# VectorE's row operations move behind the halves of a group: a parallel mixer block with a product-key expert layer

## The chip, the cores and the metric

The kernel runs on one core of a Trainium2 chip. The metric is the device time of one execution in microseconds (us): three runs of the kernel before gave 1671.1, 1673.12 and 1674.15 us, with a median of 1673.12. One further execution was taken with the hardware profiler; every row below is from it. The engines are TensorE (PE in the rows; PEld is its weight load), VectorE (DVE), ScalarE (ACT), GpSimd (POOL) and SyncE (SP), which only issues transfers.

## The reference

One layer over 512 tokens of width 1024 in float32: a convolution branch and a recurrent branch are mixed and added to `x`, and then an expert layer chooses, for each token, 128 of 16384 experts (8 heads with 16 each). The change lies in the expert layer alone, which is

```python
h = rmsnorm(x, norm_ffn_g[l])
...
def block(args):                                   # xt tokens, et their experts, gt their gates
    xt, et, gt = args
    u_sel = jnp.take(u_tab, et, axis=0)
    act = jax.nn.gelu(jnp.einsum('tkd,td->tk', u_sel, xt), approximate=False)
    v_sel = jnp.take(v_tab, et, axis=0)
    return jnp.einsum('tk,tkd->td', gt * act, v_sel)
...
return rmsnorm(x + peer_ffn(...), norm_f_g)
```

## The kernel before, in words

All the convolution, recurrence, routing and the weights of the experts are done before the main loop, which begins at about 884 us and lasts to about 1666 us of the span. Two ways of computing the expert layer run beside each other in it.

*Dense, on TensorE.* For 352 of the 512 tokens every expert is computed. The 16384 experts are 128 blocks of 128, and four blocks (`G`) are a group; the loop has 32 groups (`NG`), with numbers q from 0 to 31. For two of the four blocks the scores have been computed before the loop (`gl`, loaded from DRAM); for the other two they are computed in it (`ge`). TensorE does, for group q: `unit(q, 0)`, `unit(q, 1)`, `scores` of group q+1's third block, `unit(q, 2)`, `unit(q, 3)`, `scores` of group q+1's fourth block. A unit is 18 matmuls, a `scores` is 24 matmuls of which the last 8 read `uL`. The last group has no `scores`, and its very last unit ends with four matmuls that add the rest sum `accX` through `fold`; they wait until all row operations are done (`row_used`).

Products are done in pairs of halves: a high half made by ScalarE (`uH`, `vH`, `aH`) and a low half, the difference, made by VectorE (`uL`, `vL`, `aL`). For a block g of group q VectorE does `weigh` (writes `af`, the scores after Gelu times the gates), `v_low` (writes `vL`) and `a_low` (writes `aL`); a unit waits for `vL` and `aL`. For a block in the loop `weigh` waits for ScalarE's Gelu `ge`, and the Gelu of the fourth block waits for the `scores` that TensorE does last before `unit(q, 0)`. A `scores` waits for `u_low` (writes `uL`) before its last 8 matmuls.

*Sparse, on VectorE.* For the other 160 tokens only the chosen experts are computed: GpSimd gathers rows of `u_tab` and `v_tab` by indirect DMA, 128 rows of 4 KB at a time, into a ring of ten buffers (`ring`, `SR` is 10). In an even step VectorE does ten dot products with them (`dot`, into `spd`), ScalarE puts them through Gelu (`spg`), in the next, odd step VectorE weighs them (`gate`, writes `spa`) and adds ten gathered rows of `v_tab` times these weights into `accs` and, for the last two, `accX` (`add_row`). `row(k)` is a dot product in an even step and an addition in an odd one. Each row operation frees its buffer, and GpSimd's next gather into that buffer waits for it. An `add_row` also waits for the row operation before it:

```python
dve.wait_ge(row_used, 2 * SR * i + SR + k)
```

SyncE loads the blocks of `u_tab` and `v_tab` (512 KB each), the gates `wg` and the scores `gl` as their buffers are freed by the low halves.

Every engine executes its instructions in the order in which they are written; semaphores alone order the engines. VectorE's order for a group is written out by hand in `step`, with the row operations between the halves.

*The end.* When all row operations are done ScalarE takes the sum of squares of `accs` (`square_sum(0, DT, ...)`), and then, in this order, those of TensorE's three tiles of tokens as each is done (`tile_done`). Each is followed by a square root, VectorE's reciprocal and the last scaling into `yo`, and a store.

Of the kernel before, what the change touches and what calls it, by code (L numbers as in the profile page):

```python
# [76 lines left out]
G = 4  # L77
# [10 lines left out]
NPRE = PRE * NG  # L88
# [3 lines left out]
SR = SM + SX  # L92
# [6 lines left out]
def build(nc, xT, xR, consts, smalls, sels, reset, vecs, wlora, wall, w2a2, g2, keysT, uT, u_tab, v_tab, gfrow,  # L99
# [228 lines left out]
    with ExitStack() as ctx:  # L328
# [1371 lines left out]
        def _(dve):  # L1700
# [532 lines left out]
            def u_low(n, slot):  # L2233
                dve.wait_ge(uh_ready, n + 1)
                tt(uL[:, slot % 2, :, :], uraw[:, slot, :, :], uH[:, slot % 2, :, :], ALU.subtract).then_inc(
                    ul_ready, 1)
# [26 lines left out]
            def weigh(i, par, g):  # L2263

                q = 2 * i + par
                if g == 0:
                    dve.wait_ge(wg_loaded[par], 32 * i + 16)
                if g >= PRE:
                    dve.wait_ge(gelu_ready, NPRE + 2 * q + g - PRE + 3)
                dve.wait_ge(al_ready, G * q + g + 1)  # L2270
                src = gl[:, par, g, :] if g < PRE else ge[:, g - PRE, :]
                tt(af[:, g % 2, :].rearrange("p (b t) -> p b t", t=T_W), src.rearrange("p (b t) -> p b t", t=T_W),  # L2272
                   wg[:, par, :, g, :], ALU.mult).then_inc(act_ready, 1)

            def a_low(q, g):
                dve.wait_ge(ah_ready, G * q + g + 1)
                tt(aL[:, g, :], af[:, g % 2, :], aH[:, g, :], ALU.subtract).then_inc(al_ready, 1)

            def v_low(q, g):
                if g in POOL_V:  # L2280
                    return
                dve.wait_ge(vh_ready, G * q + g + 1)
                tt(vL[:, g, :], vraw[:, g, :], vH[:, g, :], ALU.subtract).then_inc(vl_dve, 1)  # L2283
# [4 lines left out]
            def dot(i, k):  # L2288

                dve.wait_ge(row_loaded[k], 32 * i + 16)  # L2290
                row, x = (ring[k][:, :], h2T[:, :]) if k < SM else (by_chunk_of_d(ring[k]), h2X)
                stt(row, row, 1.0, x, ALU.mult, ALU.mult, accum_out=spd[:, k:k + 1]).then_inc(row_used, 1)  # L2292

            def gate(i):
                dve.wait_ge(sp_gelu, i + 1)
                tt(spa[:, 0:SM], spg[:, 0:SM], best[:, DT].rearrange("p a b -> p (a b)")[:, bass.ds(SM * i, SM)],
                   ALU.mult)
                tt(spa[:, SM:], spg[:, SM:], gtx[:, bass.ds(SX * i, SX)], ALU.mult).then_inc(sp_gated, 1)  # L2298

            def add_row(i, k):  # L2300

                dve.wait_ge(row_loaded[k], 32 * i + 32)
                if k == 0:
                    dve.wait_ge(sp_gated, i + 1)
                dve.wait_ge(row_used, 2 * SR * i + SR + k)
                row, total = (ring[k][:, :], accs[:, :]) if k < SM else (by_chunk_of_d(ring[k]), accX)
                stt(total, row, spa[:, k:k + 1], total, ALU.mult, ALU.add).then_inc(row_used, 1)  # L2307
# [12 lines left out]
            def step(i, par, more):  # L2320
                q = 2 * i + par
                base = 2 * (1 - par)

                def row(k):
                    if par == 0:
                        dot(i, k)
                    else:
                        add_row(i, k)

                weigh(i, par, 0)  # L2330
                v_low(q, 0)
                a_low(q, 0)
                if not par:
                    row(0)
                weigh(i, par, 1)
                if not par:
                    row(1)
                v_low(q, 1)
                a_low(q, 1)
                if par:  # L2340
                    gate(i)
                    row(0)
                    row(1)
                row(2)
                weigh(i, par, 2)
                row(3)
                v_low(q, 2)
                a_low(q, 2)
                row(4)
                if more:  # L2350
                    u_low(NPRE + 2 * (q + 1), base)
                row(5)
                weigh(i, par, 3)
                v_low(q, 3)
                row(6)
                a_low(q, 3)
                row(7)
                if more:
                    u_low(NPRE + 2 * (q + 1) + 1, base + 1)
                row(8)  # L2360
                row(9)

            with dve.Fori(0, NG // 2 - 1) as i:
                step(i, 0, True)
                step(i, 1, True)
            step(NG // 2 - 1, 0, True)
            step(NG // 2 - 1, 1, False)

# [229 lines left out]
```

## Time and profile before

| | us |
|---|---|
| median of three runs (lowest, highest) | 1673.12 (1671.1, 1674.15) |
| the profiled execution, its own time | 1673.59 |
| its span | 1671.8 |
| TensorE busy in the span | 1661.5 (99%) |
| VectorE busy | 1437.0 (86%) |
| ScalarE busy | 724.1 (43%) |
| GpSimd busy | 757.7 (45%) |
| mean granted clock of TensorE | 0.998 |

The profiled execution's own time is 1.79 us over its span. The shares are those of the whole span, of which the first half is not the loop; the rows below are read by stage. A row of the timeline has a start, a duration, the engine, the line, the operation, what it writes and reads and how many instructions are merged in it, and in brackets the idle time of the engine before it with what ended it.

### The profile page before, as it was taken

Reading aid. Unit: us, or ns where it says so; the run is one execution under the profiler, and the core shown is the slowest. Engines: PE = TensorE matmul, PEld = TensorE weight load, DVE = VectorE, ACT = ScalarE, POOL = GpSimd, SP = SyncE. Lnnn points to the kernel's source line nnn. Section 1 sums busy time; section 2 is a strip of 40 time slices with the busy share of each in tenths; the row PEclk is TensorE's granted clock in tenths of the full one; section 3 lists DMA queues with packets and bytes.
Section 4 is the critical chain, followed back from the end, with each engine's and each line's share of the span. In section 5 each row is a group of like instructions: output and inputs, shape, how many; then the busy total and the mean of one; then the engine's idle time right before and its main releaser. Section 6 shows DMA issues by size and latency. Waiting matters only on the chain.

```text
span 1671.8 us, 33592 instructions
## 1 busy us (share of the span) xinstructions
PE 1661.5 (99%) x12009; PEld 1435.8 (86%) x12009; DVE 1437.0 (86%) x2759; ACT 724.1 (43%) x1053; POOL 757.7 (45%) x605
## 2 busy tenths in 40 slices
PE   9999999999999999999999999999999999999998
PEld 6878788788888999999998888888888888888886
DVE  5379988666598999999997999999999999999996
ACT  5565445453422333467774434343333333333333
POOL 0000000010054477688885665655555565555550
PEclk9999999999999999999999999999999999999999
DMA  5221122244322355578889999999999999999993
GB/s 188 79 74 53 47 90 78 84 176 149 116 81 85 131 184 175 185 223 255 253 261 367 410 410 410 410 410 410 409 394 394 385 385 383 387 384 401 393 350 112
DMA packets 166339, 424.98 MB, mean 254 GB/s; under 512 B 14160, under 2 KB 75728, under 8 KB 166000
## 3 DMA queue, kind: packets, MB, share of 16 engines
q1 hardware_dynamic: 117328, 244.52, 41.0%
q0 software_dynamic: 48928, 179.33, 27.8%
q8 instruction: 55, 0.90, 0.2%
q14 instruction: 28, 0.23, 0.0%
HBM read 382.87 MB, written 39.45 MB: 253 GB/s over the span
## 4 chain that ended last, share of the span: by engine, by line
PE 97%; ACT 1%; DVE 1%; issue 0%; DVEq 0%; ACTq 0%
PE unit L453 97%; DVE oneh L2220 0%; PE unit L608 0%; ACT L1241 0%; PE unit L1030 0%; ACT ld L1241 0%; ACT aa L1241 0%; ACT k L1241 0%; ACT best L1241 0%; ACT pk L1241 0%; DVE wL L1720 0%; ACT sqj L1241 0%; ACT wst L1241 0%; ACT kn L1241 0%; ACT uH L1241 0%
## 5 line engine op out<-in xcount | busy, mean ns | idle before, releaser
L453 PE MATMUL unit<-h2H,uH 128*128 128x352 f32 x1024 | 334.7, 328 | 0.2 <-ACTq L1572 0.2
L453 PE MATMUL unit<-h2L,uH 128*128 128x352 f32 x1024 | 328.8, 323 | 0.0
L2440 POOL DMA_INDIRECT ring<-u_tab,idx x128 | 172.6, 1348 | 156.1 <-DVE accs L2307 122.3
L453 PE MATMUL unit<-vL,aH 128*128 128x512 f32 (+1 forms) x768 | 241.7, 396 | 0.0
L453 PE MATMUL unit<-vH,aH 128*128 128x512 f32 (+1 forms) x768 | 239.4, 392 | 0.0
L453 PE MATMUL unit<-vH,aL 128*128 128x512 f32 (+1 forms) x768 | 238.9, 392 | 0.0
L2440 POOL DMA_INDIRECT ring<-v_tab,idx x128 | 172.6, 1348 | 139.1 <-DVE ring L2292 132.6
L453 PEld LDWEIGHTS unit<-h2H,uH 128*128 128x128 f32 x1024 | 192.8, 188 | 4.6 <-issue 0.4
L453 PEld LDWEIGHTS unit<-h2L,uH 128*128 128x128 f32 x1024 | 193.0, 188 | 2.8
L453 PE MATMUL unit<-h2H,uL 128*128 128x352 f32 x1024 | 191.2, 325 | 0.0
L1241 ACT ACTIVATE vH<-vraw 128x1024 fp32r<-128x1024 f32 x128 | 135.0, 1055 | 91.0 <-PE unit L453 91.0
L453 PEld LDWEIGHTS unit<-vH,aL 128*128 128x128 f32 (+1 forms) x768 | 137.8, 179 | 41.5
L453 PEld LDWEIGHTS unit<-vL,aH 128*128 128x128 f32 (+1 forms) x768 | 137.6, 179 | 40.0
L1241 ACT ACTIVATE aH<-af 128x352 fp32r<-128x352 f32 x128 | 63.4, 495 | 244.7 <-DVE af L2272 244.6
L1241 ACT ACTIVATE ge<-unit 128x352 f32<-128x352 f32 x128 | 58.7, 459 | 253.0 <-PE unit L453 252.3
L2307 DVE SCALAR_TENSOR_TENSOR accs<-ring,spa,accs 128x1024 f32<-128x1024 f32 x128 | 164.0, 1281 | 4.8 <-DVE spa L2298 3.3
L453 PEld LDWEIGHTS unit<-h2H,uL 128*128 128x128 f32 x1024 | 167.8, 189 | 0.0
L453 PEld LDWEIGHTS unit<-vH,aH 128*128 128x128 f32 (+1 forms) x768 | 135.9, 179 | 32.3
L2283 DVE TENSOR_TENSOR vL<-vraw,vH 128x1024 fp32r<-128x1024 f32 x128 | 156.0, 1219 | 8.2 <-ACT vH L1241 8.2
L2387 POOL DMA_DIRECT2D gate_dram<-gst x16 | 8.9, 555 | 332.6 <-ACT gst L1241 332.6
L2292 DVE SCALAR_TENSOR_TENSOR ring<-ring,h2T 128x1024 f32<-128x1024 f32 x128 | 155.7, 1217 | 0.3 <-DMA ring<-u_tab,idx 0.3
L2463 POOL TENSOR_SCALAR oh<-cst,e2s 128x128 f32<-128x128 f32 x176 | 136.0, 787 | 14.2 <-PE unit L453 12.9
(331 smaller groups left out, 3309.1 us busy)
## 6 DMA issues: line engine op xcount, KB each, us to landing
uraw<-uT SPq DMA_DIRECT2D x128, 512.0 KB, 6.4
vraw<-v_tab SPq DMA_DIRECT2D x128, 512.0 KB, 7.6
wraw<-wall SPq DMA_DIRECT2D x68, 512.0 KB, 3.3
w_dram<-wst SPq DMA_DIRECT2D x11, 1920.0 KB, 8.6
wg<-w_dram SPq DMA_DIRECT2D x30, 704.0 KB, 7.0
g_dram<-ge SPq DMA_DIRECT2D x64, 176.0 KB, 1.9
gl<-g_dram SPq DMA_DIRECT2D x32, 352.0 KB, 9.0
gate_dram<-gst POOLq DMA_DIRECT2D x16, 256.0 KB, 2.3
```

What stands on the lines that cost most here:

```text
L453: return pe.matmul(out, lhsT, rhs, start=start, stop=stop, skip_group_check=True)
L1241: return act.activation(out, in_, f, **kw)
L2283: tt(vL[:, g, :], vraw[:, g, :], vH[:, g, :], ALU.subtract).then_inc(vl_dve, 1)
L2292: stt(row, row, 1.0, x, ALU.mult, ALU.mult, accum_out=spd[:, k:k + 1]).then_inc(row_used, 1)
L2307: stt(total, row, spa[:, k:k + 1], total, ALU.mult, ALU.add).then_inc(row_used, 1)
L2387: pool.dma_start(gate_dram[k], gst[:, k % 2, :]).then_inc(gate_stored[k % 2], 16)
L2440: pool.indirect_dma_start(out=ring[k][:, :], out_offset=None, in_=(u_tab, v_tab)[half], in_offset=bass.IndirectOffsetOnAxis(ap=rows[:, m:m ...
L2463: ins = pool.tensor_scalar(oh2[:, b, k, :], C(C_IOTA), e2s[:, tok:tok + 1], None, ALU.is_equal)
```

## The change

`step` on VectorE is written in another order; no instruction's work is changed, and no other engine's program. Three groups of operations that stood between each other are separated: `gate` and both `u_low` come behind the four blocks' `weigh`, `v_low` and `a_low`, and the row operations behind these, all ten in an odd step (`par` is 1). In an even step four of the ten stay between the blocks, one behind each `a_low`, and six come at the end. Inside a block `v_low` stands ahead of `a_low` as before.

```diff
-                weigh(i, par, 0)
-                v_low(q, 0)
-                a_low(q, 0)
-                if not par:
-                    row(0)
-                weigh(i, par, 1)
-                if not par:
-                    row(1)
-                v_low(q, 1)
-                a_low(q, 1)
+                for g in range(G):
+                    weigh(i, par, g)
+                    v_low(q, g)
+                    a_low(q, g)
+                    if par == 0:
+                        row(g)
                 if par:
                     gate(i)
-                    row(0)
-                    row(1)
-                row(2)
-                weigh(i, par, 2)
-                row(3)
-                v_low(q, 2)
-                a_low(q, 2)
-                row(4)
                 if more:
-                    u_low(NPRE + 2 * (q + 1), base)
-                row(5)
-                weigh(i, par, 3)
-                v_low(q, 3)
-                row(6)
-                a_low(q, 3)
-                row(7)
-                if more:
-                    u_low(NPRE + 2 * (q + 1) + 1, base + 1)
-                row(8)
-                row(9)
+                    for s in range(2):
+                        u_low(NPRE + 2 * (q + 1) + s, base + s)
+                for k in range(0 if par else G, SR):
+                    row(k)
```

The first place is VectorE's last step of the program, group 31, an odd one without `u_low`. `ring_201` to `ring_204` are the last four of the ten gathered buffers. Before, from the fourth block's `weigh` to the last addition:

```order
L2272 TENSOR_TENSOR af<-ge,wg 128x352
L2283 TENSOR_TENSOR vL<-vraw,vH 128x1024
L2307 SCALAR_TENSOR_TENSOR accs<-ring_201,spa,accs 128x1024
L2277 TENSOR_TENSOR aL<-af,aH 128x352
L2307 SCALAR_TENSOR_TENSOR accs<-ring_202,spa,accs 128x1024
L2307 SCALAR_TENSOR_TENSOR accX<-ring_203,spa,accX 128x8x128
L2307 SCALAR_TENSOR_TENSOR accX<-ring_204,spa,accX 128x8x128
```

And now, from the same `weigh`:

```order
L2272 TENSOR_TENSOR af<-ge,wg 128x352
L2283 TENSOR_TENSOR vL<-vraw,vH 128x1024
L2277 TENSOR_TENSOR aL<-af,aH 128x352
L2296 TENSOR_TENSOR spa<-spg,best 128x8
L2298 TENSOR_TENSOR spa<-spg,gtx 128x2
L2307 SCALAR_TENSOR_TENSOR accs<-ring_195,spa,accs 128x1024
L2307 SCALAR_TENSOR_TENSOR accs<-ring_196,spa,accs 128x1024
L2307 SCALAR_TENSOR_TENSOR accs<-ring_197,spa,accs 128x1024
L2307 SCALAR_TENSOR_TENSOR accs<-ring_198,spa,accs 128x1024
L2307 SCALAR_TENSOR_TENSOR accs<-ring_199,spa,accs 128x1024
L2307 SCALAR_TENSOR_TENSOR accs<-ring_200,spa,accs 128x1024
L2307 SCALAR_TENSOR_TENSOR accs<-ring_201,spa,accs 128x1024
```

Behind the fourth block's `weigh` there stood four additions; now there stand all ten (the three after the last row shown are those of `ring_202`, `ring_203` and `ring_204`).

The second place is VectorE's last even step, group 30, from the third block's `weigh`. Before:

```order
L2272 TENSOR_TENSOR af<-ge,wg 128x352
L2292 SCALAR_TENSOR_TENSOR ring_198,spd<-ring_198,h2T 128x1024
L2283 TENSOR_TENSOR vL<-vraw,vH 128x1024
L2277 TENSOR_TENSOR aL<-af,aH 128x352
L2292 SCALAR_TENSOR_TENSOR ring_199,spd<-ring_199,h2T 128x1024
L2235 TENSOR_TENSOR uL<-uraw,uH 128x1024
L2292 SCALAR_TENSOR_TENSOR ring_200,spd<-ring_200,h2T 128x1024
```

And now:

```order
L2272 TENSOR_TENSOR af<-ge,wg 128x352
L2283 TENSOR_TENSOR vL<-vraw,vH 128x1024
L2277 TENSOR_TENSOR aL<-af,aH 128x352
L2292 SCALAR_TENSOR_TENSOR ring_197,spd<-ring_197,h2T 128x1024
L2272 TENSOR_TENSOR af<-ge,wg 128x352
L2283 TENSOR_TENSOR vL<-vraw,vH 128x1024
L2277 TENSOR_TENSOR aL<-af,aH 128x352
L2292 SCALAR_TENSOR_TENSOR ring_198,spd<-ring_198,h2T 128x1024
L2235 TENSOR_TENSOR uL<-uraw,uH 128x1024 x2
L2292 SCALAR_TENSOR_TENSOR ring_199,spd<-ring_199,h2T 128x1024
```

The first `uL`, for which TensorE's `scores` waits, stood behind five dot products and three blocks; now it stands behind four dot products and four blocks.

## Rows read from the trace of the kernel before

**Rows 1.** Engines in two stretches of the loop: busy time of PE, PEld, DVE, ACT, POOL; clock; DMA; GB/s
```profile
900.00:1000.00 100.00, 100.00 (x496) 84.89 (x496) 95.83 (x129) 35.39 (x52) 67.24 (x49) 1.00 1.03 410
1300.00:1400.00 100.00, 100.00 (x492) 84.32 (x491) 92.31 (x124) 35.17 (x51) 56.40 (x42) 1.00 1.00 386
```

**Rows 2.** The chain of waits: start, length, what, for the whole loop
```profile
883.68 782.54 PE unit L453 x3844
```

**Rows 3.** Timeline of PE: first matmuls of a group, of a scores, of a group
```profile
891.20 0.63 PE L453 MATMUL unit<-vH,aH 128*128 128x512 f32 x2
...
1208.38 0.62 PE L453 MATMUL unit<-vH,aH 128*128 128x512 f32 x2
...
1216.72 0.32 PE L453 MATMUL unit<-h2H,uH 128*128 128x352 f32 x1
...
1232.78 0.62 PE L453 MATMUL unit<-vH,aH 128*128 128x512 f32 x2
```

**Rows 4.** Timeline of DVE: first step, an even step, and the odd one's gate
```profile
885.80 0.53 DVE L2272 TENSOR_TENSOR af<-gl,wg 128x352 f32<-128x352 f32 x1 [1.01 <-DMA wg<-wst]
...
1217.64 0.52 DVE L2272 TENSOR_TENSOR af<-gl,wg 128x352 f32<-128x352 f32 x1
...
1219.64 1.22 DVE L2292 SCALAR_TENSOR_TENSOR ring<-ring,h2T 128x1024 f32<-128x1024 f32 x1
...
1220.79 0.52 DVE L2272 TENSOR_TENSOR af<-gl,wg 128x352 f32<-128x352 f32 x1
...
1233.56 0.53 DVE L2272 TENSOR_TENSOR af<-ge,wg 128x352 f32<-128x352 f32 x1 [1.82 <-ACT ge L1241]
1234.42 1.23 DVE L2283 TENSOR_TENSOR vL<-vraw,vH 128x1024 fp32r<-128x1024 f32 x1 [0.33 <-ACT vH L1241]
...
1246.84 0.17 DVE L2296 TENSOR_TENSOR spa<-spg,best 128x8 f32<-128x8 f32 x1 [1.03 <-ACT spg L1241]
...
1247.34 3.93 DVE L2307 SCALAR_TENSOR_TENSOR accs<-ring,spa,accs 128x1024 f32<-128x1024 f32 x3 [0.22 <-DVE spa L2298]
```

**Rows 5.** Timeline of ACT beside the same fourth block
```profile
1232.98 0.46 ACT L1241 ACTIVATE ge<-unit 128x352 f32<-128x352 f32 x1 [6.54 <-PE unit L453]
...
1235.23 0.49 ACT L1241 ACTIVATE aH<-af 128x352 fp32r<-128x352 f32 x1
```

**Rows 6.** DMA issues of 960 to 1100 us: out<-in, count, median us to landing
```profile
ring<-u_tab,idx POOLq DMA_INDIRECT x24, 18.2
```

**Rows 7.** The same of 1300 to 1500 us
```profile
ring<-u_tab,idx POOLq DMA_INDIRECT x36, 6.9
```

**Rows 8.** Timeline of DVE in its last step
```profile
1636.59 4.07 DVE L2307 SCALAR_TENSOR_TENSOR accs<-ring,spa,accs 128x1024 f32<-128x1024 f32 x3
...
1648.35 0.53 DVE L2272 TENSOR_TENSOR af<-ge,wg 128x352 f32<-128x352 f32 x1 [1.90 <-ACT ge L1241]
...
1650.45 1.28 DVE L2307 SCALAR_TENSOR_TENSOR accs<-ring,spa,accs 128x1024 f32<-128x1024 f32 x1
1651.64 0.52 DVE L2277 TENSOR_TENSOR aL<-af,aH 128x352 fp32r<-128x352 f32 x1
```

**Rows 9.** Timeline of PE: the last matmuls
```profile
1664.30 1.90 PE L453 MATMUL unit<-accX,fold 128*32 128x512 f32 x4
```

**Rows 10.** Timeline of ACT at the end
```profile
1656.16 1.06 ACT L1241 ACTIVATE sqj<-accs 128x1024 f32<-128x1024 f32 x1 [6.51 <-DVE accX L2307]
...
1657.33 1.28 ACT L1241 ACT_TABLE_LOAD   x1
1658.63 0.29 ACT L1241 ACTIVATE rsf<-ssq,vec 128x1 f32<-128x1 f32 x1
1661.62 1.03 ACT L1241 ACTIVATE sqj<-unit 128x1024 f32<-128x1024 f32 x1 [2.70 <-PE unit L453]
...
1663.02 1.03 ACT L1241 ACTIVATE sqj<-unit 128x1024 f32<-128x1024 f32 x1
...
1666.24 1.02 ACT L1241 ACTIVATE sqj<-unit 128x1024 f32<-128x1024 f32 x1 [1.78 <-PE unit L453]
```

## The prediction, made before the changed kernel was run

> **What bounds the kernel now.** I read the page first for the shares, then the engines by stretch, then the chain of waits, then the timelines of one even and one odd step, and last those of the end.
>
> In both stretches of the loop TensorE is busy for 100.00 of 100 us at a granted clock of 1.00, its full 2.4 GHz [rows 1], and the chain holds it in one unbroken piece of 782.54 us, from 883.68 to 1666.22 us [rows 2]. So the loop is TensorE's alone. From one first unit to the next is 1232.78 - 1208.38 = 24.40 us; two units take 1216.72 - 1208.38 = 8.34, so four take 16.68 and each of the two scores 3.86 [rows 3]. VectorE is at 92 to 96% in the loop [rows 1]: it isn't the bound, but has only about 2 us in 24.4 to give. The reader is to see two things. No reordering on VectorE can make the loop shorter, since TensorE does not wait there. And VectorE runs ahead: for the group that TensorE begins at 1232.78 it began at 1217.64, a lead of 15.1 us [rows 3, 4]. That lead was only 891.20 - 885.80 = 5.4 us at the first group. It ends where the fourth block's weigh must wait for the Gelu of scores which TensorE finishes just before the group (1.82 us idle, at 1233.56, 0.78 us behind TensorE's start) [rows 4].
>
> **The change, part by part.** It removes and adds no work: 10 row operations, 4 blocks and 2 uL per step, as before. Three costs are possible: TensorE waits for a half that comes later; the rows cost more when they stand together; and the last rows end later. All are worked out from the pinned point, TensorE's start B of a group.
>
> *An odd step.* The fourth weigh starts at B + 0.78, its vL at B + 1.64 [rows 4], aH ends at 1235.23 + 0.49, so B + 2.94 [rows 5], and aL, the last instruction of the blocks, at about B + 3.4. Two small multiplications of the gate take 0.50 (1246.84 to 1247.34). Then come two uL, for which I take a dot product's pitch, 1220.79 - 1219.64 = 1.15, since they work on as many elements: B + 6.2. Then ten additions. Their pitch differs by what stands between: three in a row take 3.93, of which the last is 1.28 long, so (3.93 - 1.28) / 2 = 1.33 [rows 4], while one with another instruction behind it gives way after 1651.64 - 1650.45 = 1.19 [rows 8]. An addition waits for the one before, and this wait is hidden when something else stands between. Ten together: 9 x 1.33 + 1.2 = 13.2, about 1 us more than interleaved. The step ends at B + 19.4, and VectorE begins the next, even group 24.4 - 19.4 = 5.0 us before TensorE does, no longer 15.
>
> *An even step.* Weigh, vL and aL of a block take 1219.64 - 1217.64 = 2.00 [rows 4]. The first aL is ready 2.1 us after the step's start, 2.9 us before its unit. Four blocks (8.0), four dots (4.6) and the first uL (1.2) take 13.8 us, so uL is there at 8.8 us of TensorE's group. TensorE reads it after two units and 16 of the 24 score matmuls, 8.34 + 2/3 x 3.86 = 10.9. This slack of 2.1 us is the smallest in the loop. The second block has 2.9 + 4.17 - 1.15 - 2.0 = 3.9 of slack, the later ones more. With the second uL and six dots the step ends 8.0 + 4.6 + 2.3 + 6.9 = 21.8 us after its start, and the odd step begins 24.4 + 5.0 - 21.8 = 7.6 us ahead of TensorE. Its first three blocks take 6 us, with perhaps 1 us of wait for vH, and then VectorE idles until the Gelu. So both steps are pinned again, the 1 us of dearer additions is taken from VectorE's idle time, and TensorE never waits. The leads, 5.0 and 7.6, are near the 5.4 with which the loop begins, so the start needs no time of its own. Cost of the loop: 0. The cover is 2.1 us; beyond it each late microsecond in an even step is paid 16 times.
>
> *The end.* Here nothing covers. Before, rows were done when ScalarE began to square accs, at 1656.16, long before TensorE's last matmul [rows 10]. Now the fourth weigh still starts at 1648.35 and vL ends its turn at 1650.45 [rows 8]; aL (0.45) and the gate (0.4) bring 1651.3; ten additions follow. In this step, which stands outside the loop, the pitch of dependent ones is (4.07 - 1.28) / 2 = 1.39 [rows 8], so they end at 1651.3 + 9 x 1.39 + 1.28 = 1665.1. ScalarE is then the chain: from squaring accs to its root are 1658.63 - 1656.16 = 2.47 us, with the table load of 1.28 in it that was hidden before, the root 0.29, and two tiles of 1663.02 - 1661.62 = 1.40 each [rows 10]. The third tile's square starts at 1665.1 + 2.47 + 0.29 + 2.80 = 1670.7 in place of 1666.24: 4.4 us later. The last matmuls, four of 1.90 us in all, wait for the rows too, from 1665.1 in place of 1664.30 [rows 9], but end at 1667.0, before ScalarE wants them. What lies behind the third square (root, reciprocal, scaling, store) stays, only that the stores now follow each other by 1.40 us; one of 512 KB takes 1.36 us at 386 GB/s [rows 1], so they barely queue: 0.1, with 0 to 0.5 as bounds.
>
> The Trainium skill (VectorE: DVE Perf Modes, The DRAIN you can't avoid) has it that the gap between two VectorE operations is the pipeline's own and that a semaphore on each costs nothing more. The trace has 1.39 against 1.19 for the additions that wait for each other. By the page the pitch in the end would be the shorter one; that is the second rival below.
>
> The Trainium skill (ScalarE: Activation LUTs, What ACT_TABLE_LOAD costs) charges a change of table about 2.66 us, 1.28 of load and 1.38 of drain. The load's 1.28 agrees, but the root starts 0.02 us behind it [rows 10]. If the drain came in as well now that the load is on the path, the sum would be 1.4 us more; this is the last rival.
>
> *Sum.* 4.4 + 0.1 = 4.5 us on the profiled execution's 1673.59, so 1678.1. That execution stood 0.47 over the median of the runs, so for the median 1677.6 us.
>
> **The rivals.**
>
> *Rows land too late, and TensorE starves.* A buffer freed by the first addition at about B + 7.5 is wanted by the first dot product of the even step at B + 19.4 + 2.0 = 21.4: 13.9 us for issue and landing. In 960 to 1100 us a gather landed 18.2 us after its issue [rows 6], which would be 4.3 late, 2.2 beyond the slack. In 900 to 1200 us, six pairs of steps, that is 13 us: 1691, and if it held to the end 16 x 2.2 = 35. Against it: this delay is a queue. It stood while VectorE ran faster than TensorE and pulled 410 GB/s; later, pinned, it asks for 386 and a gather lands in 6.9 us [rows 1, 7], 7 us inside the limit. The change pins VectorE from the first pairs on. If it hits the first pairs only, 2 to 7 us: about 1682. A wait of TensorE might also lower its clock, which is nowhere below 1.00 in these stretches.
>
> *The rows end early enough (the other side).* If in the last step the additions follow each other by 1.19, they end at 1651.3 + 9 x 1.19 + 1.28 = 1663.3, the third square starts at 1668.9, and the loss is 2.6 us: 1675.7, no measurable change. The point from which it decides: nothing is lost at all if the rows end by 1666.24 - 5.56 = 1660.7, and under 0.2% if by 1664.0. For it: single additions do this. Against it: the three rows in this very step did not.
>
> *A gain in the loop.* Only if TensorE had waits that the profile doesn't show; with 782.54 unbroken I give it little.
>
> *The table's drain:* 4.5 + 1.4 = 5.9, or 1679.0.
>
> **How the numbers follow.** Forecast 0.67; late rows 0.10; short pitch 0.16; gain 0.03; drain 0.04. 0.2% is 3.3 us, about what a measurement of this kernel can tell from no change; the border is 1676.5. The forecast's own spread is about 1 us each way (noise of the medians, the gate and aL read to 0.3, the stores), so a tenth of it falls within 0.2%. Slower: 0.60 + 0.10 + 0.04 = 0.74; same: 0.07 + 0.16 = 0.23; faster 0.03. The range takes in the short pitch below and the mild case of late rows above: 1675.5 to 1681.5.
>
> **What the profile after would show.** TensorE's period still 24.40, at clock 1.00, and no idle in the loop. VectorE's lead about 5 us in even and 7.6 in odd steps, and idle before the fourth weigh in odd steps only. Gathers landing in 7 to 10 us already around 1000 us. VectorE's last addition ending near 1665, ScalarE squaring accs right behind it, and the third tile's square near 1670.7. The forecast is wrong if the chain shows VectorE or a gather inside the loop, or if ScalarE's squares of the first two tiles start when their tiles are done.

## The result, and the profile after

| | before | after |
|---|---|---|
| median of the runs, us (lowest, highest) | 1672.8 (1671.1, 1674.15), 6 runs | 1679.72 (1678.54, 1680.96), 6 runs |
| ratio to before, 95% interval | | 1.0036 (1.0026 to 1.0047) |
| profiled execution, own time / span | 1673.59 / 1671.8 | 1680.04 / 1678.2 |
| VectorE, GpSimd busy | 1437.0, 757.7 | 1446.7, 724.4 |

By the ratio the change makes the kernel slower by 6.0 us (4.4 to 7.9 by the interval; the medians in the table lie 6.9 apart); the forecast was 4.5. Experiment 1 and two pairs of profiles below put the loss into the last step.

*The loop.* The engines by stretch, the same two as in [rows 1], in the profile after (busy time of PE, PEld, DVE, ACT, POOL; clock, DMA share, GB/s):

```profile
900.00:1000.00 100.00, 100.00 (x494) 84.56 (x493) 94.09 (x125) 34.70 (x51) 56.85 (x46) 1.00 1.03 410
1300.00:1400.00 100.00, 100.00 (x492) 84.38 (x491) 93.02 (x124) 35.57 (x53) 52.69 (x43) 1.00 1.01 388
```

TensorE is as full as before. Its timeline has the first unit of the first group, of an odd and an even group, the first matmul of the even group that reads `uL`, and the first unit of the last group:

```profile
892.83 0.63 PE L453 MATMUL unit<-vH,aH 128*128 128x512 f32 x2
...
1210.01 0.62 PE L453 MATMUL unit<-vH,aH 128*128 128x512 f32 x2
...
1234.41 0.62 PE L453 MATMUL unit<-vH,aH 128*128 128x512 f32 x2
...
1245.31 1.45 PE L453 MATMUL unit<-h2H,uL 128*128 128x352 f32 x8
...
1649.21 0.62 PE L453 MATMUL unit<-vH,aH 128*128 128x512 f32 x2
```

From the first unit to the last group's are 756.38 us, or 31 groups of 24.40, the period of [rows 3]. The kernel before has the same length, 1647.58 - 891.20 = 756.38; its last group begins at

```profile
1647.58 0.62 PE L453 MATMUL unit<-vH,aH 128*128 128x512 f32 x2
```

VectorE beside these groups (the `weigh` of the odd group's fourth block, its additions, the even step's first `weigh`, its `uL`, the next step's first `weigh`):

```profile
1210.79 0.53 DVE L2272 TENSOR_TENSOR af<-ge,wg 128x352 f32<-128x352 f32 x1 [1.82 <-ACT ge L1241]
...
1215.84 10.52 DVE L2307 SCALAR_TENSOR_TENSOR accs<-ring,spa,accs 128x1024 f32<-128x1024 f32 x8
...
1228.92 0.52 DVE L2272 TENSOR_TENSOR af<-gl,wg 128x352 f32<-128x352 f32 x1
...
1241.53 2.35 DVE L2235 TENSOR_TENSOR uL<-uraw,uH 128x1024 fp32r<-128x1024 f32 x2
...
1250.68 0.51 DVE L2272 TENSOR_TENSOR af<-gl,wg 128x352 f32<-128x352 f32 x1
```

The even step begins 1234.41 - 1228.92 = 5.5 us ahead of TensorE; in [rows 3, 4] this lead was 15.1. The next odd step begins 1234.41 + 24.40 - 1250.68 = 8.1 us ahead. The gathers land sooner in 960 to 1100 us (median landing times; the first was 18.2 in [rows 6]):

```profile
ring<-u_tab,idx POOLq DMA_INDIRECT x24, 8.9
ring<-v_tab,idx POOLq DMA_INDIRECT x23, 11.7
```

Ahead of that, in 884 to 960 us, those of `u_tab` still took 12.5 us, against 14.7 in the kernel before. VectorE waited for a gather three times in the whole loop, 2.8 us in all (3.7 before), and TensorE never.

*The end.* The chain of waits on the profile's page, which was TensorE for 97% of the span before, now holds nothing of TensorE (engine shares of the whole span):

```profile
DVE 1%; issue 0%; ACT 0%; DVEq 0%
```

The chain is followed back from the last instruction, and here it breaks off at the gate of the last step, at 1652.59 us; its shares say nothing of what lies ahead of that, where TensorE is as busy as before (99% of the span). What the chain does show is that the last 25 us belong to VectorE and ScalarE. VectorE, ScalarE and TensorE there:

```profile
1649.98 0.53 DVE L2272 TENSOR_TENSOR af<-ge,wg 128x352 f32<-128x352 f32 x1 [2.76 <-ACT ge L1241]
...
1652.84 11.02 DVE L2307 SCALAR_TENSOR_TENSOR accs<-ring,spa,accs 128x1024 f32<-128x1024 f32 x8
1663.97 2.67 DVE L2307 SCALAR_TENSOR_TENSOR accX<-ring,spa,accX 128x1024 f32<-128x1024 f32 x2
...
1673.90 1.41 DVE L2358 SCALAR_TENSOR_TENSOR yo<-unit,rsf,gfb 128x512 f32<-128x512 f32 x2
```

```profile
1666.68 1.06 ACT L1241 ACTIVATE sqj<-accs 128x1024 f32<-128x1024 f32 x1 [15.39 <-DVE accX L2307]
...
1667.84 1.28 ACT L1241 ACT_TABLE_LOAD   x1
1669.14 0.29 ACT L1241 ACTIVATE rsf<-ssq,vec 128x1 f32<-128x1 f32 x1
1669.34 1.00 ACT L1241 ACTIVATE sqj<-unit 128x1024 f32<-128x1024 f32 x1
...
1671.99 1.00 ACT L1241 ACTIVATE sqj<-unit 128x1024 f32<-128x1024 f32 x1
```

```profile
1666.70 1.90 PE L453 MATMUL unit<-accX,fold 128*32 128x512 f32 x4 [0.70 <-DVE accX L2307]
```

Before, ScalarE squared `accs` at 1656.16 and then waited for TensorE's tiles [rows 10]. Now it starts at 1666.68 with all tiles but the last finished, and nothing between the square of `accs` and the third tile's waits for TensorE. TensorE's last group began 1.63 us later in this profile (1649.21 against 1647.58), so the comparison is made from there: the third square starts 22.78 us behind it, where it was 1666.24 - 1647.58 = 18.66: 4.12 us. From that square to the end of the span are 1678.2 - 1671.99 = 6.21 us against 5.56: 0.65 more. Together 4.8. The other 1.6 of the spans' 6.4 lies ahead of the loop.

Of the 0.65, 0.24 is VectorE's: its last scaling starts 1673.90 - 1671.99 = 1.91 behind the square, where it was 1667.91 - 1666.24 = 1.67, because it is still scaling the second tile. The kernel before has for the same scaling

```profile
1667.91 1.41 DVE L2377 SCALAR_TENSOR_TENSOR yo<-unit,rsf,gfb 128x512 f32<-128x512 f32 x2
```

The other 0.41 lies behind the scaling. The last two stores, halves of the third tile, land 2.5 us (median) after their issue where they took 2.0; first the kernel before, then the change:

```profile
y<-yo SPq DMA_DIRECT2D x2, 256.0 KB, 2.0
...
y<-yo SPq DMA_DIRECT2D x2, 256.0 KB, 2.5
```

### The profile page after: what moved, and what is told of

The parts are those of the page before. It is cut to its first block and busy times, and to the rows that moved or that the text cites. A ratio compares the mean times of both kernels' runs of the same rounds, so it can differ in the third digit from the quotient of the medians.

```text
span 1678.2 us, 33592 instructions
## 1 busy us (share of the span) xinstructions
PE 1661.5 (99%) x12009; PEld 1436.5 (86%) x12009; DVE 1446.7 (86%) x2759; ACT 717.3 (43%) x1053; POOL 724.4 (43%) x605
## 5 line engine op out<-in xcount | busy, mean ns | idle before, releaser
L2421 POOL DMA_INDIRECT ring<-v_tab,idx x128 | 186.0, 1453 | 154.1 <-DVE ring L2292 135.5
L2421 POOL DMA_INDIRECT ring<-u_tab,idx x128 | 142.8, 1116 | 195.2 <-DVE accs L2307 143.2
L2292 DVE SCALAR_TENSOR_TENSOR ring<-ring,h2T 128x1024 f32<-128x1024 f32 x128 | 152.2, 1214 | 1.5 <-DMA ring<-u_tab,idx 1.5
L2412 POOL TENSOR_TENSOR uL<-uraw,uH 128x1024 fp32r<-128x1024 f32 x42 | 113.8, 2712 | 61.2 <-ACT uH L1241 61.2
```

What stands on the lines that cost most here:

```text
L2412: pool.tensor_tensor(uL[:, slot % 2, :, :], uraw[:, slot, :, :], uH[:, slot % 2, :, :], ALU.subtract).then_inc(ul_ready, 1)
L2421: pool.indirect_dma_start(out=ring[k][:, :], out_offset=None, in_=(u_tab, v_tab)[half], in_offset=bass.IndirectOffsetOnAxis(ap=rows[:, m:m ...
```

## The experiments

The experiments ran in three series, each on one chip and with the kernel before in it, and a ratio is to the runs of that kernel in the same series. The change itself ran again only in the first series (experiments 1 to 3), where it measured 1.0033. Experiments 4 to 7 are compared with that number across series. Where the text adds up a trace, it takes two stretches as above: from TensorE's first unit of the last group to the third tile's square (18.66 in the kernel before), and from there to the end of the span (5.56).

**1. The last step alone, both ways.** The new order everywhere but in the last step:

```diff
-                for g in range(G):
-                    weigh(i, par, g)
-                    ...
+                if more:
+                    ...                       # the new order
+                else:
+                    ...                       # the order of before
```

> The new order in all steps but the last (group 31), which has the order of before. Theory of the end (the loss is the ten additions behind the last block, which put ScalarE's squares behind them): no loss, within 1.5 us of before; the third tile's square again right behind its last matmul. Rival, the loop or what lies ahead of it (TensorE began the last group 1.6 us later in the profile of the change): 1.5 to 2 us slower than before, with no waits in the end.

Measured 1.0005 (0.9996 to 1.0014). And the reverse, the old order everywhere but in the last step:

> The order of before in all steps but the last (group 31), which has the new one. Theory of the end: the whole loss, 4.8 us over before (4.1 until the third square starts, 0.65 behind it). Rival, loop or before it: 4.8 less than the change as a whole by 1.5 to 2, so about 3 to 4 over before if the change as a whole is 6.

Measured 1.0034 (1.0022 to 1.0046), beside 1.0033 (1.0021 to 1.0045) for the whole change in the same series. In the profile of this second kernel the third square starts 22.79 us behind the last group's start and the span ends 6.27 later, as in the change. So the last step makes the whole loss by itself, and the 31 reordered steps alone cost 0.05%, at most 0.14%. The rival, a part in the loop or ahead of it, falls by the traces: from the first unit to the last group's are 756.37 us in both kernels, and the end of the second costs 4.8. The intervals by themselves (-0.7 to 2.3 us for the first kernel) would still admit its 1.5 to 2.

The first kernel's profile has something that I did not look for. TensorE's first unit of its last group, and ScalarE at its end:

```profile
1650.23 0.62 PE L453 MATMUL unit<-vH,aH 128*128 128x512 f32 x2
...
1663.60 1.06 ACT L1241 ACTIVATE sqj<-accs 128x1024 f32<-128x1024 f32 x1 [6.25 <-DVE accX L2307]
...
1666.26 1.01 ACT L1241 ACTIVATE sqj<-unit 128x1024 f32<-128x1024 f32 x1
...
1668.92 1.00 ACT L1241 ACTIVATE sqj<-unit 128x1024 f32<-128x1024 f32 x1
```

The rows end 1663.60 - 1650.23 = 13.4 us behind the start of the group, where in the kernel before they ended 8.6 behind it, although the last step is the same. The short lead is carried into the last step: VectorE arrives late and has no idle time left in it. The third square still starts 18.7 us behind TensorE's start, just as before, but the three squares now follow each other without a gap, so by these rows any later end of the rows would move it. And what lies behind it is already dearer: from the third square to the end of the span are 1675.2 - 1668.92 = 6.28 us in place of 5.56, with scalings and stores as close together as in the change. So by the trace the reordered loop is not quite free: its shorter lead costs 0.7 us in the end even with the old last step, which agrees with the 1.0005 (0.8 us) measured. The whole change has the same 0.7 once, not twice.

**2. The change once more, and the kernel before once more.**

> The change once more, as it is. Theory of the end: 4.8 us over before, plus noise of about 1. Rival with a part ahead of the end: 6 again, and in the profile TensorE's last group again begins 1.6 us later than in the kernel before, at about 1649.2 us. If that start lies elsewhere this time, it is a difference between executions.

> The kernel before once more, for a second profile. If the 1.6 us by which the last group began later in the profile of the change is a difference between executions, this one may begin its last group anywhere from about 1647 to 1650 us, with the main loop's length unchanged; if it belongs to the change, it begins at 1647.6 again.

The change: 1.0033 (1.0021 to 1.0045); its profile has 891.50 for the first unit of the loop and 1647.87 for the first unit of the last group, 756.37 between them. The kernel before, one execution of 1674.32 us:

```profile
891.93 0.63 PE L453 MATMUL unit<-vH,aH 128*128 128x512 f32 x2
...
1656.89 1.06 ACT L1241 ACTIVATE sqj<-accs 128x1024 f32<-128x1024 f32 x1 [6.52 <-DVE accX L2307]
...
1666.97 1.02 ACT L1241 ACTIVATE sqj<-unit 128x1024 f32<-128x1024 f32 x1 [1.78 <-PE unit L453]
```

In this second pair the loop of the change begins 0.43 us before that of the kernel before (891.50 against 891.93), in the first pair it began 1.63 after it (892.83 against 891.20). Over all twelve profiles of this study the first unit starts between 889.84 and 893.86 us, in kernels whose instructions ahead of it are the same. So the 1.6 us are a difference between executions and no fixed cost of the change. Two profiles of the kernel before are too few to say whether the changed ones begin later by some tenths on average.

The end costs the same in both pairs. In the second profile of the kernel before the last group begins at 1648.30, and the third square follows 18.67 behind it; in the change's second profile the third square is at 1670.66, 22.79 behind the last group's start. From there to the end of the span are 5.53 and 6.24: together 4.8 again.

**3. The order of ScalarE's squares.**

```diff
-            act.wait_ge(row_used, P // SM * 2 * SR)
-            square_sum(0, DT, accs[:, :])
-            for t in range(DT):
-                act.wait_ge(tile_done, t + 1)
-                square_sum(t + 1, t, ...)
+            for n, t in enumerate((0, 1, DT, 2)):
+                if t == DT:
+                    act.wait_ge(row_used, P // SM * 2 * SR)
+                else:
+                    act.wait_ge(tile_done, t + 1)
+                square_sum(n, t, ...)          # DT is accs
```

The same order is given to VectorE's scaling and SyncE's stores, in two lines left out here.

> The change, with ScalarE squaring tiles 0 and 1 first, then accs, then tile 2 (VectorE's scaling and the stores in the same order). Theory of the end: the table load and two squares go back under TensorE's last matmuls; rows still end 17.4 us behind TensorE's start of the group, accs is squared from there, tile 2 1.4 later, 0.9 later than in the kernel before: 1 to 1.5 us over before, 3.3 less than the change. Rival, that the rows' end itself or the last four matmuls that wait for it are the loss: no more than 1 us less than the change.

Its profile has, for TensorE's first unit of the last group and its last matmuls, and for ScalarE's third tile:

```profile
1649.45 0.62 PE L454 MATMUL unit<-vH,aH 128*128 128x512 f32 x2
...
1666.94 1.90 PE L454 MATMUL unit<-accX,fold 128*32 128x512 f32 x4 [0.69 <-DVE accX L2309]
```

```profile
1668.88 1.02 ACT L1242 ACTIVATE sqj<-unit 128x1024 f32<-128x1024 f32 x1
```

Measured 1.0016 (1.0007 to 1.0025), 2.7 us over before and 2.8 under the change of the same series. The mechanism holds: rows end as late as in the change, and half of the loss is gone or more, because two squares are done before the rows end or beside them. The third tile's square starts 1668.88 - 1649.45 = 19.43 us behind the group's start, 0.77 later than before; that part was forecast well. The expected 1 to 1.5 us over before was low by the part behind it: 1675.5 - 1668.88 = 6.62 us from that square to the end, as against 5.56, 0.6 of it because VectorE is still scaling `accs` (its last scaling starts 2.29 us behind the square, not 1.67). By the trace the kernel is 1.8 us over before, within the interval of the runs (1.2 to 4.2).

**4. The table load.**

```diff
+            fn(rsf[:, 0:1], vc("eps", 0), ACT.Sqrt)
             def square_sum(n, t, src):
```

> The change, with one square root of a constant on ScalarE behind its last aH, so that the table of the root is loaded while the rows are still added. Theory of the end: 1.3 us less than the change (the load alone, its drain is not on the path), so 3.5 us over before, and the third tile's square starts 4.0 us behind the accs square in place of 5.3. Rival, the drain belongs to the load: 2.7 less. Rival, the load comes back at the next square: no gain.

```profile
1650.77 1.28 ACT L1241 ACT_TABLE_LOAD   x1
...
1666.15 1.06 ACT L1241 ACTIVATE sqj<-accs 128x1024 f32<-128x1024 f32 x1 [13.88 <-DVE accX L2309]
...
1667.53 1.00 ACT L1241 ACTIVATE sqj<-unit 128x1024 f32<-128x1024 f32 x1
...
1670.35 1.00 ACT L1241 ACTIVATE sqj<-unit 128x1024 f32<-128x1024 f32 x1
```

Measured 1.0021 (1.0012 to 1.0030). From the accs square to the third tile's are 4.20 us, against 1671.99 - 1666.68 = 5.31 with the load in between: 1.1 less, near the load's 1.28 and far from 2.7. Between the accs square and the first tile's the whole 1.28 is gone (1667.53 - 1666.15 = 1.38 in place of 1669.34 - 1666.68 = 2.66); 0.15 comes back between the next two, for a reason that I did not find. The load is not done again. No drain was on the path: in the change the root starts 0.02 us behind the load. By the trace the kernel is 3.5 us over before (21.68 and 6.05), as forecast. The times, also 3.5 us, agree with that, but 0.12% under the change's 1.0033 of another series could not have told 1.1 from 2.7.

**5. Both.** The early load with the order of experiment 3.

> The same early load, and ScalarE squares tiles 0 and 1 first, then accs, then tile 2. Theory of the end: accs is squared right behind the rows (17.5 us behind TensorE's start of the group) and tile 2 1.3 us later, 0.1 to 0.2 later than in the kernel before; VectorE's scaling and the stores, closer together, add 0.6 to 0.9: within 1.1 us of before, 3.7 less than the change. Rival, the rows themselves are the loss through the last four matmuls: still 2 us or more over before.

```profile
1666.24 1.06 ACT L1242 ACTIVATE sqj<-accs 128x1024 f32<-128x1024 f32 x1 [0.59 <-DVE accX L2311]
...
1668.20 1.02 ACT L1242 ACTIVATE sqj<-unit 128x1024 f32<-128x1024 f32 x1 [0.49 <-PE unit L454]
```

Measured 1.0007 (0.9998 to 1.0016), 1.2 us. The detail I had wrong: the third square was to follow at once, and it waits 0.49 us for TensorE. The last four matmuls wait for the rows as well, end 1.90 us after them, and now that ScalarE is out of the way they are what is late. The third square so starts 1668.20 - 1648.77 = 19.43 us behind the group's start, where 0.1 to 0.2 over 18.66 was expected, and the span ends 6.60 behind it: 1.8 us over before by the trace, the same as experiment 3 with its 19.43 and 6.62. There ScalarE and the last four matmuls (1666.94 + 1.90 = 1668.84) are ready together, so taking the load away uncovers nothing but them. That the early load adds to the order of experiment 3 is therefore not shown: the 1.5 us between the two ratios lie within their intervals, and the traces have none of it. Some three fifths of the loss are gone by the trace, four fifths by the runs, without moving a row. This kernel isn't faster than the one before either, and none in this study is.

**6. How long additions take side by side.** In the last step alone:

```diff
-            def add_row(i, k):
+            def add_row(i, k, place=None, back=0):
...
-                dve.wait_ge(row_used, 2 * SR * i + SR + k)
+                dve.wait_ge(row_used, 2 * SR * i + SR + (k if place is None else place) - back)
...
+                if not more:
+                    for place, k in enumerate((0, 8, 1, 9, 2, 3, 4, 5, 6, 7)):
+                        add_row(i, k, place, 1 if 0 < place < 5 else 0)
+                    return
```

> The change, with the ten additions of the last step alone in another order: rows 0, 8, 1, 9, 2 and then the rest, so that neighbours write different sums, and each of the second to fifth waits only for the addition before the last. Theory that the longer pitch is the wait for the neighbour's end: those four start 1.2 us after their neighbour instead of 1.39, and accs is squared 0.8 us earlier. Rival, that the gap belongs to two long operations back to back whatever they wait for: 1.39 for all. The time moves by less than 1 us either way.

```profile
1652.49 1.29 DVE L2307 SCALAR_TENSOR_TENSOR accs<-ring,spa,accs 128x1024 f32<-128x1024 f32 x1
1653.69 1.28 DVE L2307 SCALAR_TENSOR_TENSOR accX<-ring,spa,accX 128x1024 f32<-128x1024 f32 x1
1654.89 1.28 DVE L2307 SCALAR_TENSOR_TENSOR accs<-ring,spa,accs 128x1024 f32<-128x1024 f32 x1
1656.09 1.28 DVE L2307 SCALAR_TENSOR_TENSOR accX<-ring,spa,accX 128x1024 f32<-128x1024 f32 x1
1657.28 8.22 DVE L2307 SCALAR_TENSOR_TENSOR accs<-ring,spa,accs 128x1024 f32<-128x1024 f32 x6
```

The four that don't wait for their neighbour start 1.20 us after it; the six that do take 8.22, or (8.22 - 1.28) / 5 = 1.39 each. `accs` is squared 13.05 us behind the first addition in place of 13.84: 0.8 less, as expected. The edit changes two things for these four at once, the wait and the sum that is written. The change's own rows part them: its ninth addition writes the other sum but waits, and it starts 1663.97 - 1662.58 = 1.39 behind the eighth, which ends the 11.02 us of the eight (1652.84 + 11.02 - 1.28 = 1662.58). So it is the wait for the neighbour's end that makes the pitch, 0.19 us each time. The time was 1.0020 (1.0010 to 1.0030), 3.3 us over before, 2.2 under the change's 1.0033 and so past the 1 us that was expected at most. The trace has 4.0 over before (22.00 and 6.24) and 0.8 under the change; the intervals, of two series, overlap, and I read no more into it.

**7. Where the loop's edge is.** More dot products ahead of the `uL` of even steps:

```diff
+                late = 0 if par else 1         # 3 in the second kernel
+                for k in range(G, G + late):
+                    row(k)
                 if more:
                     for s in range(2):
                         u_low(NPRE + 2 * (q + 1) + s, base + s)
-                for k in range(0 if par else G, SR):
+                for k in range(0 if par else G + late, SR):
                     row(k)
```

> The change, with one more dot product ahead of the two uL of every even step (five instead of four), so uL comes 1.15 us later. Theory of the slack (TensorE wants uL 2.1 to 2.5 us after it is ready): still inside, 0 beside the change, and TensorE's groups still begin 24.40 us after each other. Rival, that the loop has no such edge, since VectorE's lead makes up for any order: also 0.

Measured 1.0038 (1.0027 to 1.0048), beside the change's 1.0033 in another series: no difference that the runs can tell. The trace has a little: TensorE waited once for `uL`, 0.53 us at 950.17, and from the first unit to the last group's are 757.12 us, 0.7 more than in the change. The end is that of the change (22.79 and 6.25).

> The change, with three more dot products ahead of the two uL of every even step (seven instead of four), so uL comes 3.45 us later. Theory of the slack: 0.95 to 1.35 us beyond it in each of 16 even steps, 15 to 22 us slower than the change, and TensorE idle before the last third of the scores. Rival, no edge, the lead makes up for it: 0.

Measured 1.0147 (1.0127 to 1.0166), 19 us more than the change. The waits of the loop that name `uL` (total us, times, longest), and two of them, two groups apart, in TensorE's timeline:

```profile
PEld unit L453 <- DVE uL L2235: 19.4, 16, 3.6
...
PE unit L453 <- DVE uL L2235: 14.8, 16, 3.3
```

```profile
1204.33 1.55 PE L453 MATMUL unit<-h2H,uL 128*128 128x352 f32 x8 [0.77 <-DVE uL L2235]
...
1254.16 1.55 PE L453 MATMUL unit<-h2H,uL 128*128 128x352 f32 x8 [0.77 <-DVE uL L2235]
```

Sixteen waits, one in each even step, and a pair of groups takes 1254.16 - 1204.33 = 49.83 us in place of 48.8. From the first unit to the last group's are 775.23 us, 18.85 more than in the change: about 15 times 1.03, and 3.4 for the first pair, where TensorE waits 3.3 us. Of three more dot products, 3.45 us, 1.03 is paid, so the slack was about 2.4, within the 2.1 to 2.5 expected, and behind it nothing is made up. The granted clock stayed at 1.00 in the two stretches of the loop that were read (900 to 1000 and 1300 to 1400 us), waits and all.

## Why the prediction was right, step by step

- *TensorE alone bounds the loop, and it never waits.* Right: period 24.40 and no wait in the loop, and the last step alone gives the whole loss (experiment 1). What the forecast did not have is that the shorter lead reaches into the end by itself: 0.7 us with the old last step.
- *The leads.* 5.0 and 7.6 us were forecast, 5.5 and 8.1 measured. The slack of the first `uL` was put at 2.1; it is ready at 1241.53 + 1.2 = 1242.7 and read at 1245.31, so 2.6. Both are 0.5 off for one reason: the odd step ends sooner than I added it up. The gate's two multiplications take 0.15 before the first `uL` starts (1213.42 to 1213.57), not the 0.50 after which additions follow, and the ten additions take 0.1 less.
- *Ten additions cost 13.2.* 1215.84 to 1228.92: 13.1. In the last step 13.84 to the square, of the 13.8 forecast.
- *The end.* The third square 4.4 later was forecast and 4.1 measured: between the squares that do not wait for TensorE lie 1.33 us, not the 1.40 of [rows 10], and the root and the next square overlap by 0.09.
- *Behind the third square*, 0.1 us was forecast, with 0.5 as the bound; it is 0.65, and 0.7 in the second pair. This is the term that was mis-sized, and it lies beyond its own bound. Two things add up in it: VectorE's last scaling starts 0.24 later behind the square, and 0.4 lies in the stores, whose last halves land 0.5 us later after their issue. That they do so because they stand closer together is my reading; every other kernel of this study but the one before has the 2.5 us too, but none moves the stores alone.
- *The sum*: 4.5 forecast; the traces give 4.8; the runs give 6.0, 5.5 and, for the last step alone, 5.7. The intervals reach down to 3.5 to 4.4, so 4.8 is in all of them. All three runs' values lie above it. Part of that lies outside the spans: in the series of experiment 1 the medians of the spans are 1672.2 before, 1677.45 for the change and 1677.8 for the last step alone, 5.3 and 5.6 apart. The rest was not settled; the start of the loop, which moves by up to 4 us between executions, is larger than it.
- *The rivals.* Late rows: TensorE never waited for them. Landings were 8.9 us in place of 18.2, as argued, since VectorE no longer runs ahead, though not from the first pairs on (12.5 us up to 960 us), and those of `v_tab` took 11.7, more than the 7 to 10 forecast for all. Shorter pitch: refuted by the 1.39, and experiment 6 shows why the single addition has 1.20. The table's drain: refuted by experiment 4. A gain in the loop: none.

## What to carry to other kernels

An engine that is not the bound may be put in another order for nothing in the loop as long as each result still comes before it is wanted; that can be worked out from the timeline. Here 1.15 us later cost 0.7 us in the whole loop, 3.45 us later cost 19. But the last round has no next round to hide in. Whatever is moved to the end of a step is paid there, and all that waits behind it is uncovered with it (here two squares, a table load, four matmuls and the stores). Look at the lead, too, with which the engine enters the last round. Write the last round by itself (0.8 us left of the loss), or let what follows take first what is ready first (1.8 left by the trace).

## What the runs showed of the hardware that was not expected

- A VectorE addition of 128x1024 elements that waits for the end of the one ahead starts 1.39 us after it; one that waits only for the one before that starts 1.20 us after its neighbour. In the loop of the program (`Fori`) the eight additions of a step take 10.52 us, a pitch of 1.32, though each waits for its neighbour too; why it is shorter there was not looked into.
- GpSimd's gathers of 512 KB from `u_tab` landed after 18.2 us (median) in 960 to 1100 us when VectorE ran ahead of TensorE there, and after 8.9 us when it was held to TensorE's pace, at almost the same rate (410 and 408 GB/s). The longer time is therefore, as I read it, waiting in the queue and not a slower transfer; no run takes the queue apart.
- A table load on ScalarE takes 1.28 us, and the root behind it starts 0.02 us later. Moved under VectorE's rows, it gave back 1.28 us between the two squares that it stood between.
- Executions differ by up to 4 us in when the loop begins (889.84 to 893.86 in twelve profiles), while from the first unit to the last group's it took 756.37 or 756.38 us in the ten profiles without a wait for `uL`. For a loss of 5 us the two pairs of profiles, read from a fixed point of the loop, gave 4.8 both times, where the two intervals for the change are 3.5 and 4.0 us wide.
